# A transformer step on one core: another order of loading, modulating and norming at its beginning

## The chip, the core and the metric

One core of a Trainium2 chip runs the whole step as one program. The metric is the device time of one execution in microseconds; the kernel before took 1898.06 us, the median of three executions. The engines are TensorE (PE, with its weight loads as PEld), VectorE (DVE), ScalarE (ACT), GpSimd (POOL) and SyncE (SP), which here issues the DMAs.

## The reference, cut to what matters

640 tokens of width 1024 (512 latent, 128 context) go through two layers. Each layer begins with a norm that is modulated by vectors computed from a conditioning, one for the latent tokens (`c`) and one for the context tokens (`c_ctx`):

```
def modulation(cond, w_ada, b_ada):
    m = jax.nn.silu(cond) @ w_ada + b_ada          # (6 * 1024)
    return m.reshape(cond.shape[0], 6, D_MODEL)

def modulate(x, g, shift, scale):
    return rms_norm(x, g) * (1 + scale[:, None, :]) + shift[:, None, :]

hp = modulate(xp, g[0], mc[:, 0], mc[:, 1])
hs = modulate(xs, g[0], ml[:, 0], ml[:, 1])
...   # h @ w_in (1024 x 3584), retention and attention heads, @ w_out, MLP; then layer 1
```

The change concerns the part up to the first tiles of `h @ w_in`: shift and scale of layer 0, which are the first 2048 columns of `w_ada[0]`, the first norm, and `h` itself.

## The kernel before

Activations are kept transposed: `xT` has eight tiles `k` (feature groups of 128 on the partitions) by 640 tokens, and tokens are worked in two halves `s` of 320; the second half holds 192 latent and 128 context tokens, so its modulation has two pieces (`HALVES`). Every large matmul is done in float32 by three passes: an operand is split into `hi` (a rounding copy) and `lo` (the difference), and `unit` (lines 733 to 752) adds `lo*hi`, `hi*lo`, `hi*hi` over the eight `k` for both halves, 48 matmuls of 320 columns a unit. Weights come in pieces of 512 KB into four stage buffers (`load_piece`), ACT makes `w_hi` (`act_split`, line 535), DVE `w_lo` (`dve_split`, line 544). Stage "ac" has 20 such units; piece `n + 2` is split once unit `n` is done, since two slots hold the split pieces. Beside these units DVE accumulates the later modulation vectors from `w_ada` slabs (`ada_ops`, lines 1945 and 1948), and PE sums them over partitions (`sum_rows`, line 788: four matmuls of 32 columns of weights and 512 moving columns, one for each 32-column group of the array).

The program of each engine is written out by hand, so the order on an engine is the order of the text. The beginning is:

- SP issues the constants and small vectors, three 1 MB loads of `w_ada` (`load_ada`, line 554; 256 columns of all 1024 rows, so rows of 1 KB), the tokens `xtok` (lines 635, 636), five more loads of `w_ada` as the ring of three comes free, then the first four pieces, two slabs and, after the last ada step, the table `dist`.
- PE transposes the small vectors, does `ada_step(0..2)` (eight matmuls of two weight columns, `csil`, by 256 moving columns each, line 822; a small transpose of the result follows, `turn_mod`, line 812), then the 40 transposes of the tokens (line 840), ada steps 3 to 5, the sums of squares of half 0 (`sum_squares`, lines 761 and 765), step 6, those of half 1, step 7, and `spread_root` for both (line 775). Then come the units.
- ACT copies each step's result (`mod_rows`, line 1424), squares the tiles (line 1357), takes the roots (line 1364), splits pieces 0 and 1, and does `first_operand` (line 1369).
- DVE copies the transposed tokens (lines 1969, 1971), adds the bias to each step's columns (`mod_columns`, line 1913), splits pieces 0 and 1, and then does `first_modulate` for each `k` and both halves in turn (lines 1851 and 1854).
- POOL adds the squares (line 2465) and makes the low part of each tile (`first_low`, line 2469).

In unit 0 `both_ready` makes PE wait for tile `k` of both halves. Later norms ("in0m", "in1", "in1m") work by halves with `modulate` on DVE, `operand` on ACT and `low` on DVE, beside other units.

Of the kernel before, what the change touches and what calls it, by code (L numbers as in the profile page):

```python
# [19 lines left out]
P = 128  # L20
D = 1024
# [181 lines left out]
ADA_W = 256  # L203
N_ADA = 2 * 6 * D // ADA_W
ADA_RING = 3
ADA_START = 8
# [42 lines left out]
def build(nc, i, o):  # L249

    top = ExitStack()
    with top:
# [64 lines left out]

        [ada_a] = lay(64, ("ada_a", [P, ADA_RING, KD, ADA_W], F32))
        [modrow_a] = lay(130, ("modrow_a", [2, 2, ADA_W], F32))

# [58 lines left out]
        ada_in = [sem(f"ada_in{n}") for n in range(ADA_RING)]  # L379
# [110 lines left out]
        def norm_place(name, s, k):  # L490

            n = 2 * (k % 2) + s if name == "in0" else k % 4
            return nt[:, n // 2, HALF * (n % 2):HALF * (n % 2 + 1)]
# [56 lines left out]

        def load_ada(queue, n):

            src = i["w_ada"][0].rearrange("(k p) m -> p k m", p=P)
            queue.dma_start(ada_a[:, n % ADA_RING], src[:, :, ADA_W * n:ADA_W * (n + 1)])\
                .then_inc(ada_in[n % ADA_RING], 16)
# [27 lines left out]
        def _(sp):  # L583
# [64 lines left out]
            sp.wait_ge(ada_done, ADA_START)  # L648
# [69 lines left out]
        def _(pe):  # L718
# [14 lines left out]
            def unit(name, u, k_tiles, m, x_hi, x_lo, ready=None, base=0, wide=None, beside=None):  # L733

                wide = wide or m
                g, n, (_, only) = UNIT_AT[name] + u, PIECE_AT[name] + unit_piece(name, u), unit_tile(name, u)
                pe.wait_ge(w_lo_done, n + 1)
# [3 lines left out]
                for j, k in enumerate(range(k_tiles)):  # L741
# [4 lines left out]
                    for s in range(2) if only is None else (only,):  # L746
# [5 lines left out]
                last.then_inc(unit_done, 1)  # L752
# [53 lines left out]
            def turn_mod(n):  # L806
                pe.wait_ge(modrow_done, n + 1)
                if n >= 2:
                    pe.wait_ge(mod_out, n - 1)
                modrow = modrow_a  # L810
                for j in range(2):
# [4 lines left out]
            def ada_step(n):  # L816
# [8 lines left out]
                if n:  # L825
                    turn_mod(n - 1)
# [1846 lines left out]
```

## Time and profile before

| | |
|---|---|
| median of three executions | 1898.06 us (1897.71 to 1900.3) |
| the profiled execution | 1896.75 us, span 1895.0 us |
| mean granted TensorE clock | 0.959 |
| busy in the span | PE 94%, DVE 57%, ACT 39%, POOL 12% |
| first tile of the first norm starts on DVE | 60.77 us |
| unit 0 done, unit 1 done | 84.7 us, 92.6 us |

The profiled execution is one execution; its span is measured from the first to the last instruction, and 1.75 us of its time lie around the span. Times in the rows below are microseconds from the span's start. A busy share is an average over stages with different limits; for a change at the beginning the rows of the beginning count, and what comes after only tells whether a shift is kept. A wait is put down to the semaphore that came last.

### The profile page before, as it was taken

To read this page: it belongs to the slowest core of one execution; us is meant where nothing else is said; L and a number is where in the kernel's file an instruction comes from. 1 tells how busy PE (TensorE), PEld (TensorE's weight loads), DVE (VectorE), ACT (ScalarE), POOL (GpSimd) and SP (SyncE) were. 2 spreads that over 40 slices of the span, in tenths; PEclk is the share of its full clock that TensorE was granted. 3 is DMA by queue.
4 is the path that set the end of the run, shared out by engine and by line. 5 is a ranking of instruction groups with operands and counts; after the bars stand their busy time and mean duration, and the time that the engine had idled before them with its cause. 6 is when DMAs were issued, how large, how long until landed. Compare 5 with 4: busy or idle time off the path is not lost.

```text
span 1895.0 us, 27246 instructions
## 1 busy us (share of the span) xinstructions
PE 1776.7 (94%) x11072; PEld 1568.8 (83%) x11072; DVE 1080.2 (57%) x1716; ACT 734.1 (39%) x1235; POOL 224.5 (12%) x234
## 2 busy tenths in 40 slices
PE   7799997789999999999998998999899999999997
PEld 3699872358999999999998996333699999999997
DVE  2567836763556677777454655566555673342345
ACT  1323215364554321312334464555446532131232
POOL 1300000142200000000121030333221000000012
PEclk9799999889999999999997998999999999999998
DMA  8354322103236546555310030000314552222231
GB/s 270 102 168 155 111 67 67 34 1 90 64 104 185 171 122 193 150 159 154 98 43 25 26 109 1 1 1 1 112 34 123 177 147 78 77 69 78 79 90 56
DMA packets 262447, 179.46 MB, mean 95 GB/s; under 512 B 12862, under 2 KB 236979, under 8 KB 262323
## 3 DMA queue, kind: packets, MB, share of 16 engines
q1 hardware_dynamic: 262322, 177.72, 32.1%
q8 instruction: 88, 1.44, 0.3%
q14 instruction: 37, 0.30, 0.1%
HBM read 174.15 MB, written 3.62 MB: 94 GB/s over the span
## 4 chain that ended last, share of the span: by engine, by line
PE 84%; DVE 6%; ACT 4%; issue 3%; POOL 2%; DMA 0%; SPq 0%; DVEq 0%; ACTq 0%; POOLq 0%
PE ps L749 22%; PE ps L751 21%; PE ps L750 21%; PE ps L1268 3%; PE ps L822 2%; PE ps L1278 2%; PE ps L765 1%; PE ps L883 1%; PE ps L884 1%; PE ps L885 1%; PE ps L775 1%; PE ps L1179 1%; PE ps L761 1%; ACT km L1715 1%; PE ps L897 1%
## 5 line engine op out<-in xcount | busy, mean ns | idle before, releaser
L535 ACT ACTIVATE w_hi<-stage 128x1024 fp32r<-128x1024 f32 (+1 forms) x177 | 185.5, 1050 | 679.2 <-PE ps L751 550.3
L544 DVE TENSOR_TENSOR w_lo<-stage,w_hi 128x1024 fp32r<-128x1024 f32 (+1 forms) x177 | 218.4, 1236 | 341.1 <-ACT w_hi L535 340.9
L749 PE MATMUL ps<-hM_hi,w_lo 128*128 128x320 f32 x960 | 300.9, 313 | 2.4 <-DVE hM_lo L1879 2.4
L750 PE MATMUL ps<-hM_lo,w_hi 128*128 128x320 f32 x960 | 299.0, 311 | 0.0
L751 PE MATMUL ps<-hM_hi,w_hi 128*128 128x320 f32 x960 | 299.0, 311 | 0.0
L749 PE MATMUL ps<-h_hi,w_lo 128*128 128x320 f32 x824 | 257.8, 313 | 2.6 <-DVE h_lo L2262 2.6
L750 PE MATMUL ps<-h_lo,w_hi 128*128 128x320 f32 x824 | 256.2, 311 | 0.0
L751 PE MATMUL ps<-h_hi,w_hi 128*128 128x320 f32 x824 | 256.1, 311 | 0.0
L2465 POOL TENSOR_TENSOR rstd<-rstd,sq 128x320 f32<-128x320 f32 x80 | 80.6, 1014 | 1046.9 <-ACT sq L1357 1044.1
L749 PEld LDWEIGHTS ps<-hM_hi,w_lo 128*128 128x128 f32 x960 | 182.5, 190 | 6.8 <-DVE hM_lo L1879 3.5
L750 PEld LDWEIGHTS ps<-hM_lo,w_hi 128*128 128x128 f32 x960 | 182.5, 190 | 0.0
L751 PEld LDWEIGHTS ps<-hM_hi,w_hi 128*128 128x128 f32 x960 | 182.4, 190 | 0.0
L749 PEld LDWEIGHTS ps<-h_hi,w_lo 128*128 128x128 f32 x824 | 156.3, 190 | 6.6 <-DVE h_lo L2262 3.7
L750 PEld LDWEIGHTS ps<-h_lo,w_hi 128*128 128x128 f32 x824 | 156.3, 190 | 0.0
L751 PEld LDWEIGHTS ps<-h_hi,w_hi 128*128 128x128 f32 x824 | 156.2, 190 | 0.0
L1948 DVE SCALAR_TENSOR_TENSOR acc_mlp<-slab_mlp,csil,acc_mlp 128x512 f32<-128x512 f32 x196 | 134.5, 745 | 0.0
L749 PE MATMUL ps<-hA_hi,w_lo 128*128 128x320 f32 x320 | 103.4, 323 | 9.9 <-POOL hA_lo L2469 9.9
L2245 DVE TENSOR_TENSOR yT<-yT,ps 128x640 f32<-128x640 f32 (+1 forms) x64 | 41.8, 653 | 123.1 <-PE ps L751 122.5
L750 PE MATMUL ps<-hA_lo,w_hi 128*128 128x320 f32 x320 | 101.8, 318 | 0.0
L751 PE MATMUL ps<-hA_hi,w_hi 128*128 128x320 f32 x320 | 101.8, 318 | 0.0
L2355 DVE TENSOR_REDUCE w_lo<-ps 128x1 fp32r<-128x640 f32 x64 | 52.1, 814 | 66.5 <-PE ps L1180 46.1
L1767 ACT ACTIVATE pT<-ps 128x512 f32<-128x512 f32 x84 | 50.0, 596 | 76.5 <-PE ps L1268 73.9
(363 smaller groups left out, 3606.7 us busy)
## 6 DMA issues: line engine op xcount, KB each, us to landing
stage<-in_w_mlp_out SPq DMA_DIRECT2D x83, 512.0 KB, 4.4
stage<-in_w_mlp_in SPq DMA_DIRECT2D x80, 512.0 KB, 4.3
slab_mlp<-in_w_ada SPq DMA_DIRECT2D x28, 1024.0 KB, 5.3
stage<-in_w_in_ac SPq DMA_DIRECT2D x28, 512.0 KB, 3.8
slab_ac<-in_w_ada SPq DMA_DIRECT2D x12, 1024.0 KB, 6.5
ada_a<-in_w_ada SPq DMA_DIRECT2D x8, 1024.0 KB, 8.1
stage<-in_w_out_ac SPq DMA_DIRECT2D x8, 512.0 KB, 4.4
stage<-in_w_out_c SPq DMA_DIRECT2D x8, 512.0 KB, 4.1
```

Of the source, the lines that this page charges most:

```text
L535: nc.scalar.activation(hi_place(n)[:, 0:width], stage[:, n % STAGE, 0:width], ACT.Copy)\
L544: nc.vector.tensor_tensor(lo_place(n)[:, 0:width], stage[:, n % STAGE, 0:width], hi_place(n)[:, 0:width].bitcast(F32), ALU.subtract).then_ ...
L749: mm(out, lo[:, k], xh, start=j == 0, stop=False)
L750: mm(out, hi[:, k], xl, start=False, stop=False)
L751: last = mm(out, hi[:, k], xh, start=False, stop=j == k_tiles - 1)
L822: last = mm(ps[0:2, n % 2, 0:ADA_W], csil[:, k, :], slot[:, k, :], start=k == 0, stop=k == KD - 1)
L1268: mm(ps[:, 2 + n % 2, :], km[0:97, h, P * kb:P * (kb + 1)], q, start=True, stop=True).then_inc(m_s, 1)
L1767: f(pT[:, n % P_RING, :], ps[:, 2 + n % 2, :], ACT.Exp).then_inc(m_e, 1)
L1948: last = stt(acc, w, c, acc, ALU.mult, ALU.add)
L2245: tt(y_, y_, p_, ALU.add).then_inc(dve_evac, 1)
L2355: nc.vector.tensor_reduce(peak[p % 2][:, 96 + j:97 + j], src, AX.X, ALU.max, negate=True).then_inc(a_max, 1)
L2465: sub(rstd[:, half(s)], rstd[:, half(s)], sq[:, k % 2, half(s)], ALU.add).then_inc(added[s], 1)
```

## The change

- SP: the tokens are issued right behind the small vectors. Then come eight loads of `w_ada`, one for each `k`: 128 rows of 2048 columns (8 KB a row), 1 MB each, each with its own semaphore and place, no ring. The four first pieces follow, then the small decay inputs, the slabs, and `dist`, which waits for nothing now.
- PE: the tokens' transposes come first. `ada_step(k)` is four matmuls, one for each 32-column group, with 32 weight columns (`cwide`: two used, thirty zero) and 512 moving columns, accumulated over `k` in one bank. Steps 0 to 5 stand behind the transposes, 6 and 7 between the sums and the spreads. Then four 128x128 transposes turn the whole result at once.
- ACT makes one copy of 128x512 where it made eight of 2x256; the squares of both halves stand one behind the other; the second piece's split stands behind tile 3 of half 0.
- DVE: one `first_columns` in place of eight `mod_columns`. The first norm's tiles go by halves with the functions of the later norms; `first_modulate`, `first_operand`, `first_low` go. Split 0 stands behind the second tile, split 1 behind the sixth. Before half 1, DVE waits for its own eight low parts of half 0.
- PE does unit 0 and unit 1 of stage "ac" for half 0, then both for half 1 (`part`).
- POOL gains one memset (`cwide`) and loses sixteen subtractions.

The diff, without lines that follow from these:

```diff
-            for n in range(ADA_RING):
-                load_ada(sp, n)
             sp.dma_start(xtok[:, 0:NB, :], i["x_sample"][0].rearrange("(b p) d -> p b d", p=P)).then_inc(x_in, 16)
             sp.dma_start(xtok[:, NB, :], i["x_prompt"][0]).then_inc(x_in, 16)
+            for k in range(KD):
+                sp.dma_start(ada_a[:, k, :], i["w_ada"][0, P * k:P * (k + 1), 0:4 * GRP]).then_inc(ada_in[k], 16)
+            for j in range(STAGE):
+                load_piece("ac", j)
...
-            for n in range(ADA_RING, ADA_START):
-                sp.wait_ge(ada_done, n - ADA_RING + 1)
-                load_ada(sp, n)
-            for j in range(STAGE):
-                load_piece("ac", j)
             load_slab(0)
             load_slab(1)
             table_rows()
-            sp.wait_ge(ada_done, ADA_START)
...
+            def ada_step(k):
+                pe.wait_ge(ada_in[k], 16)
+                for j in range(4):
+                    last = mm(ps[32 * j:32 * j + 32, 0, :], cwide[:, k, :], ada_a[:, k, GRP * j:GRP * (j + 1)],
                               start=k == 0, stop=k == KD - 1)
+                if k == KD - 1:
+                    last.then_inc(ada_done, 1)
...
+            pe.wait_ge(c_ready, 1)
+            for k in range(6):
+                ada_step(k)
             pe.wait_ge(x_out, 10)
-            ada_step(5)
             sum_squares("in0", 0)
             ada_step(6)
             sum_squares("in0", 1)
+            spread_root("in0", 0)
             ada_step(7)
-            spread_root("in0", 0)
             spread_root("in0", 1)
+            pe.wait_ge(modrow_done, 1)
+            for n in range(4):
+                last = nc.tensor.transpose(ps[:, 1, P * n:P * (n + 1)], modrow_a[:, P * n:P * (n + 1)], ident[:])
+            last.then_inc(mod_t, 1)
...
-            for j in range(20):
-                unit("ac", j, KD, P, hA_hi, hA_lo, ready=both_ready if j == 0 else None)
+            for s in range(2):
+                for j in range(2):
+                    unit("ac", j, KD, P, hA_hi, hA_lo, ready=h_ready("in0", s) if j == 0 else None, part=s)
+            for j in range(2, 20):
+                unit("ac", j, KD, P, hA_hi, hA_lo)
...
             square_root("in0", 0, D)
             square_root("in0", 1, D)
-            mod_rows(7)
+            act.wait_ge(ada_done, 1)
+            f(modrow_a[:], ps[:, 0, :], ACT.Copy).then_inc(modrow_done, 1)
             act_split(act, 0)
-            act_split(act, 1)
             for k in range(KD):
-                for s in range(2):
-                    first_operand(s, k)
+                operand("in0", 0, k)
+                if k == 3:
+                    act_split(act, 1)
+            for k in range(KD):
+                operand("in0", 1, k)
...
+            first_columns()
+            modulate("in0", 0, 0)
+            modulate("in0", 0, 1)
             dve_split(dve, 0)
-            dve_split(dve, 1)
+            low("in0", 0, 0)
+            for k in range(2, KD):
+                modulate("in0", 0, k)
+                low("in0", 0, k - 1)
+                if k == 5:
+                    dve_split(dve, 1)
+            low("in0", 0, KD - 1)
+            dve.wait_ge(h_lo_done[0], KD)
             for k in range(KD):
-                for s in range(2):
-                    first_modulate(s, k)
+                modulate("in0", 1, k)
+                if k:
+                    low("in0", 1, k - 1)
+            low("in0", 1, KD - 1)
```

## Rows read from the trace of the kernel before

**Rows 1.** The page: busy time of the engines and their share of the span.
```profile
PE 1776.7 (94%) x11072; PEld 1568.8 (83%) x11072; DVE 1080.2 (57%) x1716; ACT 734.1 (39%) x1235; POOL 224.5 (12%) x234
```
**Rows 2.** Windows: length; busy (count) of PE, PEld, DVE, ACT, POOL; granted clock, DMA, GB/s.
```profile
65.00:82.70 17.70, 13.58 (x42) 11.01 (x43) 15.63 (x32) 6.12 (x13) 12.89 (x14) 0.50 0.01 3
82.70:86.50 3.80, 3.80 (x14) 3.80 (x15) 0.67 (x1) 1.65 (x2) 0.00 (x0) 0.50 0.00 0
...
160.00:200.00 40.00, 40.00 (x276) 38.96 (x275) 31.59 (x45) 11.49 (x15) 0.00 (x0) 1.00 0.51 159
```
**Rows 3.** Timeline: start, duration, engine, line, operation; first tile, splits behind units 0, 1.
```profile
60.77 0.48 DVE L1851 TENSOR_TENSOR nt<-xT,ps 128x320 f32<-128x320 f32 x1
...
84.74 1.06 ACT L535 ACTIVATE w_hi<-stage 128x1024 fp32r<-128x1024 f32 x1 [3.12 <-PE ps L751]
...
92.67 1.06 ACT L535 ACTIVATE w_hi<-stage 128x1024 fp32r<-128x1024 f32 x1 [6.28 <-PE ps L751]
```
**Rows 4.** Groups by line and form, DVE, 60 to 84: busy us, mean ns.
```profile
L1854 DVE TENSOR_SCALAR nt<-nt,coef,mod 128x128 f32<-128x128 f32 x8 | 7.1, 884 | 0.0
```
**Rows 5.** The chain that ended last, 30 to 66 us: start, duration, what.
```profile
44.66 1.65 PE ps L765 x12
...
53.49 3.56 PE ps L822 x16
...
58.49 2.36 DVE w_lo L544 x2
```
**Rows 6.** Timeline of SP's DMA issues, and the landing times of xtok's two.
```profile
3.74 2.46 SPq L554 DMA_DIRECT2D ada_a<-in_w_ada  x3
6.24 3.06 SPq L635 DMA_DIRECT2D xtok<-in_x_sample  x1
...
DMA to landing us min/median/max: 12.7/13.5/14.3
```
**Rows 7.** Windows as in rows 2: ada rows, token rows, pieces of 512-byte rows.
```profile
8.00:14.00 6.00, 4.45 (x11) 1.39 (x12) 0.00 (x0) 0.00 (x0) 0.00 (x0) 1.00 1.09 349
14.00:20.00 6.00, 6.00 (x27) 2.25 (x26) 0.23 (x2) 0.75 (x2) 0.00 (x0) 1.00 1.04 407
...
42.00:48.00 6.00, 4.14 (x23) 2.96 (x24) 0.00 (x0) 3.44 (x9) 4.01 (x5) 0.80 1.20 293
```
**Rows 8.** Timeline: the tokens' first transposes and the last two copies.
```profile
23.11 2.51 PE L840 MATMUL ps<-ident,xtok 128*128 128x128 f32 x20
...
31.25 1.26 DVE L1971 COPY xT<-ps 128x512 f32<-128x512 f32 x2
```
**Rows 9.** Timeline of ACT: first and last square of half 1, then the table load.
```profile
44.39 0.45 ACT L1357 ACTIVATE rstd<-xT 128x320 f32<-128x320 f32 x1
...
50.18 0.47 ACT L1357 ACTIVATE sq<-xT 128x320 f32<-128x320 f32 x1 [0.54 <-POOL rstd L2465]
...
51.61 1.28 ACT L1364 ACT_TABLE_LOAD   x1
```
**Rows 10.** Timeline of PE: `sum_rows`, between units and after a pause.
```profile
141.79 1.07 PE L788 MATMUL ps<-acc_ac,ones 128*32 128x512 f32 x8
...
226.08 1.62 PE L788 MATMUL ps<-acc_ac,ones 128*32 128x512 f32 x8 [3.52 <-issue]
```
**Rows 11.** Timeline: a later `spread_root`; and the page: a copy-like activation from PSUM.
```profile
537.86 1.54 PE L775 MATMUL ps<-ident,rs 128*128 128x128 f32 x6 [2.57 <-DVE rs L1828]
...
L1767 ACT ACTIVATE pT<-ps 128x512 f32<-128x512 f32 x84 | 50.0, 596 | 76.5 <-PE ps L1268 73.9
```
**Rows 12.** Timeline of a later norm: half 0's tile pace on DVE, half 1's on ACT.
```profile
499.31 0.54 DVE L1866 SCALAR_TENSOR_TENSOR nt<-xT,coef,ps 128x320 f32<-128x320 f32 x1
...
500.24 0.54 DVE L1866 SCALAR_TENSOR_TENSOR nt<-xT,coef,ps 128x320 f32<-128x320 f32 x1
...
545.99 0.92 ACT L1383 ACTIVATE nt<-nt,mod,coef 128x192 f32<-128x192 f32 x2
546.95 0.47 ACT L1387 ACTIVATE hM_hi<-nt 128x320 fp32r<-128x320 f32 x1
```

More of the change, by code:

```diff
@@ L202 @@
 P_RING = 8
[L203 to L206, printed above, removed]
+ADA_START = 1
 GRP = 512
@@ L378, in build @@
         const_in, rows_in, x_in = sem("const_in"), sem("rows_in"), sem("x_in")
-        ada_in = [sem(f"ada_in{n}") for n in range(ADA_RING)]
+        ada_in = [sem(f"ada_in{k}") for k in range(KD)]
+        csil_zero = sem("csil_zero")
         decay_in, dist_in = sem("decay_in"), sem("dist_in")
@@ L731, in free_pair, with unit @@
                         pe.wait_ge(dve_evac, d)
-            def unit(name, u, k_tiles, m, x_hi, x_lo, ready=None, base=0, wide=None, beside=None):
+            def unit(name, u, k_tiles, m, x_hi, x_lo, ready=None, base=0, wide=None, beside=None, part=None):
                 wide = wide or m
                 g, n, (_, only) = UNIT_AT[name] + u, PIECE_AT[name] + unit_piece(name, u), unit_tile(name, u)
+                halves = (0, 1) if only is None and part is None else (only if part is None else part,)
                 pe.wait_ge(w_lo_done, n + 1)
@@ L745, in unit @@
                         ready(k, j)
-                    for s in range(2) if only is None else (only,):
+                    for s in halves:
                         out = ps[0:m, first_bank(g) + (s if only is None else 0), 0:HALF]
@@ L751, in unit @@
                         last = mm(out, hi[:, k], xh, start=False, stop=j == k_tiles - 1)
-                last.then_inc(unit_done, 1)
+                if part != 0:
+                    last.then_inc(unit_done, 1)
             def sum_squares(name, s):
@@ L1365, in square_root @@
                     .then_inc(root_done[s], 1)
[L1367 to L1369 removed]
             def operand(name, s, k):
                 layer, which, shift = MODULATED[name]
[L1375 removed]
+                place, out = norm_place(name, s, k), hA_hi if name == "in0" else hM_hi
                 act.wait_ge(h_full[s], KD * MOD_NO[name] + k + 1)
                 if s == 0:
[L1378 removed]
+                    f(out[:, k, half(0)], place, ACT.Identity, bias=mod[:, layer, 8 * shift + k, 0:1])\
                         .then_inc(h_hi_done[0], 1)
@@ L1385, in operand @@
                 last.then_inc(affine_done, 1)
-                act.wait_ge(affine_done, KD * (MOD_NO[name] - 1) + k + 1)
-                f(hM_hi[:, k, half(1)], place, ACT.Copy).then_inc(h_hi_done[1], 1)
+                act.wait_ge(affine_done, KD * MOD_NO[name] + k + 1)
+                f(out[:, k, half(1)], place, ACT.Copy).then_inc(h_hi_done[1], 1)
             def y_square(name, stage, u):
@@ L1843, in residual @@
                 tt(xT[:, k, cols], xT[:, k, cols], place, ALU.add).then_inc(x_done[s], 1)
-            def first_modulate(s, k):
-                dve.wait_ge(rstd_done[s], 1)
-                if k >= 2:
-                    dve.wait_ge(h_lo_done[s], k - 1)
-                place = norm_place("in0", s, k)
-                link(tt(place, xT[:, k, half(s)], spread("in0", s), ALU.mult))
-                for a, b, g in HALVES[s]:
-                    part = place[:, a - HALF * s:b - HALF * s]
-                    last = ts(part, part, coef[:, 0, A1, k, g:g + 1], mod[:, 0, 8 * SHIFT1 + k, g:g + 1],
-                              ALU.mult, ALU.add)
-                last.then_inc(h_full[s], 1)
             def modulate(name, s, k):
@@ L1957, in _ @@
             link(nc.vector.reciprocal(cexp[:], cexp[:]))
+            dve.wait_ge(csil_zero, 1)
+            for g in range(2):
+                tt(cwide[:, :, g], vecT[:, ROW_C + 8 * g:ROW_C + 8 * g + 8], cexp[:, 8 * g:8 * g + 8], ALU.mult)
             for g in range(2):
@@ L2474, in _ @@
                     add_square("in0", s, k)
-            for k in range(KD):
-                for s in range(2):
-                    first_low(s, k)
             pool.wait_ge(v_done, 8)
```

91 lines of the change are left out of this document (17 added, 74 removed).

## The prediction

> **What bounds the kernel now.** I read the page first: TensorE (PE) is busy 94% of the span [rows 1]. Then the windows by stage: a steady stretch behind the beginning has PE busy 40.00 of 40 us, at the full clock, with 276 matmuls (0.145 us each), while DVE has room (31.59) [rows 2]. The change touches only what lies ahead of it. So from the third projection unit on, the kernel is PE-bound, and whatever the beginning saves shifts everything behind it. The stretch to price ends when unit "ac" 1 ends: ACT starts piece 3's split, which waits for exactly that, at 92.67; unit 0 ended before 84.74 [rows 3].
>
> Next the timeline and the chain, backwards from 92.6. Units 0 and 1 hold 96 matmuls; at 0.145 they need 14 us, but unit 0 alone takes from 65 to 84.6. It waits, tile by tile, for the DVE, ACT, GpSimd round of `first_modulate`, `first_operand`, `first_low`, and since PE pauses it holds the lower level: granted clock 0.50 (1.2 GHz) from 65 to 86.5, busy 13.58 of 17.70 us [rows 2]. A 128-column `tensor_scalar` of this round takes 0.884 us while GpSimd works [rows 4]. In front of the round, first tile at 60.77 [rows 3], stands a chain of four ada steps behind the squares, the last of 3.56 us, and then two splits on DVE (2.36 us) [rows 5]. Before that, PE could start only when tokens landed: they are queued behind 3 MB of modulation weights and land 12.7 to 14.3 us after their issues, the first at 6.24 [rows 6].
>
> **Part 1, tokens first.** The token issue takes the place of the first ada issue, 3.74 instead of 6.24 [rows 6], and nothing large is ahead of it. 4 KB rows (14 to 20 us) came at 407 GB/s, 1 KB rows (8 to 14) at 349 [rows 7]. 2.6 MB plus the small vectors at 407 take 6.7 us from about 4.7, plus about 1 us until a semaphore is seen (the first 5.4 MB at these rates end near 19.7 and the tokens' landing reads 20.5): 12.4. At 349 it would be 13.6. The ten groups of transposes and their copies are DVE-bound; from the first transpose at 23.11 to the last copy's end at 32.51 [rows 8] they take 9.4 us; PE may be at the slow level, which costs the first group 0.3: xT is ready at 22.2.
>
> The Trainium skill ("DMA: Bandwidth & Descriptors", Specifications) gives about 358 GB/s as a core's limit from HBM. The trace moves 407 in a six-microsecond stretch [rows 7], so the measurement decides; by the page's figure the tokens would land 1.1 us later and the time would be about 2 us higher than my forecast.
>
> **Part 2, squares.** They no longer wait for ada rows. One half takes 6.3 us, from the first square at 44.39 to the end of the last at 50.65, bound by GpSimd's adds between them [rows 9]. Two halves back to back: 22.2 + 12.6 = 34.8. ACT's table load of 1.28 follows (as at 51.61) [rows 9]: 36.1; square root and reciprocal 0.4: 36.5.
>
> **Part 3, modulation vectors.** Removed: 8 steps of 8 matmuls, 8 small copies, 16 small transposes. Added: 8 steps of 4 matmuls with 32 weight columns each, in four column groups. The nearest row is `sum_rows`, same shape and groups: its 4 matmuls (8 records) last 1.07 us, and 1.62 in a stretch at the slow level [rows 10]. Streamed one behind the other, the same 2048 columns are the old step, 3.56 [rows 5]. I take 1.0 to 1.6 a step. Rows of 8 KB should come no slower than 4 KB ones: 2.6 us for 1 MB, the last at 12.4 + 8 x 2.6 = 33.2 (36.4 or later at 349, with the later tokens 37.6). PE is in order: transposes until 22, steps 0 to 5 until 29.6 (row 5 lands at 28), sums 0, step 6, sums 1 (2.2 us each; their later part takes 1.65) [rows 5] until about 35.3, so ACT's squares and table load end last, not DMA. Then, in a line: spread 0 from 36.5, 1.0 (1.54 for such six records at the slow level) [rows 11], to 37.6; step 7, 1.3, to 38.9; ACT's copy of 128x512, 0.6 [rows 11], beside spread 1, to 39.9; four transposes, 0.5 to 1.0 with what a hand-over costs (20 take 2.51 at the full clock) [rows 8], to 40.8; two adds and two coefficients on DVE, 0.7, first `modulate` at 41.5, against 60.77: 19.3 us saved so far. ACT's first split comes behind the copy and is hidden beside the transposes; its piece lands behind all ada rows and about 1.8 us (512 KB at 293) [rows 7] later, at 35 to 39.5. SP's queue passes eight 1 MB issues before pieces 0 to 3, the decay vectors, slabs and `dist`; the last of 16 MB has landed by 53 even at 293, and the slabs' first reader comes at 68.
>
> **Part 4, tiles by halves.** Half 0 is later layers' pattern: one modulate plus one low per tile, 0.93 us (499.31 to 500.24) [rows 12]. Two modulates, split 0 (1.15), low: 2.6. Six pairs 5.6, split 1 1.15, last low 0.5: 9.9 us; unit 0's first half runs along, and unit 1's first half, which the old order had no room for, starts then. The new self-wait before half 1 holds DVE for about 0.1, nothing is queued behind it but these tiles. Half 1 is ACT-bound: two affine pieces and a copy, 545.99 to 547.42, 1.43 a tile [rows 12]; 0.5 + 8 x 1.43 + 0.7 = 12.6. Total 22.5 us against 21.8 in the old round: this part saves nothing on the tiles themselves. It saves behind them, since half of unit 1 is already done. After the last tile 27 matmuls are left instead of 51. In the old round PE, once fed without pause, stood at 0.50 for 3.8 us more (82.7 to 86.5, 14 matmuls) [rows 2]; so 14 in 3.8 us and 13 at 0.145: 5.7 us. Unit 1 ends at 41.5 + 22.5 + 5.7 = 69.7.
>
> Is the next unit ready? Unit 0 is done near 65; ACT's split and DVE's, 2.5 us, end at 67.5, and the bank's copy is done by then: PE goes on without a gap. GpSimd loses 16 operations that nobody misses.
>
> **Sum.** 92.6 - 69.7 = 22.9 us. The profiled execution took 1896.75 us (span 1895.0): 1873.9. It stands 1.3 below the median of 1898.06; with that, 1875.2. Unknowns: DMA at 349 throughout delays sums 1 and step 7 and costs 3; a full clock from the ada steps on would give 1.4 before the tiles and 1.7 after them, a slow one costs 1.2 before them; one tile of half 1 waiting longer costs under 2; where the clock falls and rises later, about 1 either way. Down they add up to 4.1, up to 6.2 or 7: 1871 to 1881.5.
>
> **Rivals.** (a) *The head comes out slower than its rows*: the long rows arrive at 293 GB/s like the pieces [rows 7], PE does steps late, tiles take one wait more each: 6 to 10 us less gain, 1881.5 to 1885. Against it: rates grow with the row length in this trace. (b) *Column groups do not run side by side*: PE is the bound. Steps run back to back from 22.2, ada is done at 22.2 + 5.4 + 8d, against 38.9. With d = 3.6: 17.5 us lost, gain 5.4, 1892.7. (c) *The other side*: the same, at the slow level. Zero gain is at d = 4.3 us a step; with 7.1 (2 x 3.56) it is 1898.06 + 22.6 = 1920.7. Against (b) and (c): 1.07 and 1.62 us in [rows 10]; for them only that the old beginning has no such matmul. (d) *The gain is real but is given back*: a stage that waits for a transfer with a fixed time. All later loads wait on progress, not on time, and the beginning's are landed 20 us before their readers: 1897 to 1899.
>
> **Chances.** Forecast 0.85 (of which 0.05 below 1871, with the fast clock), (a) 0.08, (b) 0.02, (c) 0.03, (d) 0.02. The range holds about 0.80. Something like 0.2% (3.8 us) is what a measurement of this kernel can tell from no change. Faster by more: 0.95; same: 0.02; slower: 0.03.
>
> **What would show it.** In the profile after: x_sample lands near 12, last xT copy ends near 22; groups of 8 ada records last 1.0 to 1.7 us and wait for DMA; last square ends near 35; first modulate near 41.5; low of half 0 paces 0.93, half 1 1.43; the split of piece 3 starts at 69.7 instead of 92.67, and PE is full from there on. A last ada row after 38, ada groups of 3 us and more, or PE gaps between units 1 and 3 would make me wrong.

## The result and the profile after

The changed kernel took 1882.42 us (median of five, 1874.76 to 1883.39), the kernel before 1899.59 us beside it; the ratio is 0.9905 with a 95% interval of 0.9885 to 0.9925. It is faster by 17 to 18 us, not by 22.9, and 0.9 us slower than the upper end of the range. The profiled execution took 1881.38 us. Of the runs below, one execution of the run both took 1992.44 us at a mean granted clock of 0.82, where all others have 0.955 to 0.965; it is left out of every figure.

The page of after, for [rows 1]: engines' busy time, and the queue that brings the engines' own instructions, which [rows 1] does not show; its line is the same in both. (Its columns: packets, MB, share of 16 engines.)
```profile
PE 1756.4 (93%) x10996; PEld 1562.0 (83%) x10996; DVE 1073.5 (57%) x1696; ACT 738.8 (39%) x1244; POOL 209.7 (11%) x219
...
q8 instruction: 88, 1.44, 0.3%
```
The timeline of after from the tokens' landing to the first tile, for [rows 5, 6, 8, 9, 11]: start, duration, engine, line, operation.
```profile
13.05 4.83 PE L814 MATMUL ps<-ident,xtok 128*128 128x128 f32 x28 [7.26 <-DMA xtok<-in_x_prompt]
...
21.68 1.27 DVE L1925 COPY xT<-ps 128x512 f32<-128x512 f32 x2
...
25.48 1.06 PE L802 MATMUL ps<-ada_a,cwide 128*32 128x512 f32 x8 [1.24 <-DMA ada_a<-in_w_ada]
...
27.97 1.06 PE L802 MATMUL ps<-ada_a,cwide 128*32 128x512 f32 x8 [1.42 <-DMA ada_a<-in_w_ada]
...
32.08 1.93 PE L802 MATMUL ps<-ada_a,cwide 128*32 128x512 f32 x8
...
35.17 1.41 PE L753 MATMUL ps<-ones,rstd 128*128 128x1 f32 x6 [1.15 <-POOL rstd L2424]
35.54 1.28 ACT L1341 ACT_TABLE_LOAD   x1
36.44 2.70 PE L757 MATMUL ps<-ones,sq 128*128 128x1 f32 x12
...
39.00 1.52 PE L767 MATMUL ps<-ident,rs 128*128 128x128 f32 x6
...
40.45 1.94 PE L802 MATMUL ps<-ada_a,cwide 128*32 128x512 f32 x8
42.32 1.45 PE L767 MATMUL ps<-ident,rs 128*128 128x128 f32 x6
...
43.60 0.61 PE L829 MATMUL ps<-ident,modrow_a 128*128 128x128 f32 x4
...
44.82 1.01 DVE L1818 SCALAR_TENSOR_TENSOR nt<-xT,coef,ps 128x320 f32<-128x320 f32 x2
```
The reader sees a beginning that runs 0.7 us behind the forecast up to the last square (xT ready at 22.95, forecast 22.2; table load at 35.54, forecast 34.8) and then loses 2.6 us more, so that the first tile starts 3.3 us late (44.82, forecast 41.5): from 35.17 to 44.2 one TensorE operation follows another, each at nearly twice its short duration (an ada step is 1.06 at 26 and 28, and 1.93 at 32 and 40). The windows of after, for [rows 2, 7], say why: length; busy (count) of PE, PEld, DVE, ACT, POOL; granted clock, DMA, GB/s.
```profile
16.00:32.00 16.00, 12.52 (x94) 7.14 (x92) 6.95 (x9) 5.09 (x12) 6.02 (x7) 0.93 1.00 417
...
30.00:42.00 12.00, 10.85 (x51) 7.66 (x50) 0.35 (x2) 4.58 (x10) 4.31 (x5) 0.50 1.07 292
42.00:46.00 4.00, 2.21 (x14) 1.66 (x10) 1.68 (x7) 2.15 (x4) 0.00 (x0) 0.81 1.05 396
46.00:57.00 11.00, 8.51 (x28) 7.18 (x29) 9.60 (x18) 5.86 (x12) 0.00 (x0) 0.54 0.43 139
57.00:70.00 13.00, 10.51 (x56) 9.22 (x56) 7.43 (x15) 10.78 (x24) 0.00 (x0) 0.89 0.01 2
```
The granted clock is 0.50 (1.2 GHz) for the whole stretch 30 to 42. (The clock's own records begin only at 16.2 us in after and at 14.8 in before, and the windows read 1.00 ahead of them, as the first one of [rows 7] does. How fast TensorE runs there has to be read from durations, see before_fill below.) The tiles follow: half 0 from 44.82 to 55.11, half 1 to 66.9, and the split behind unit 1 at 72.78 (timeline of ACT), for [rows 3, 12]:
```profile
60.95 0.92 ACT L1356 ACTIVATE nt<-nt,mod,coef 128x192 f32<-128x192 f32 x2
...
62.28 0.92 ACT L1356 ACTIVATE nt<-nt,mod,coef 128x192 f32<-128x192 f32 x2
...
72.78 1.06 ACT L534 ACTIVATE w_hi<-stage 128x1024 fp32r<-128x1024 f32 x1 [3.33 <-PE ps L742]
```
Unit 1 ends 19.9 us earlier than before, but the span is only 15.4 us shorter (1895.0 less 1879.6). So 4.5 us go behind the beginning. ACT's weight splits are the same in every kernel here, so the n-th split serves as a milestone. The table holds, for each kernel run, how much earlier than in the kernel before it starts (us; the head row is that split's time in the trace of before). It is worked out from the start times in the timelines. Each row is one execution, and executions of one kernel differ: after's five go from 1874.76 to 1883.39. By the span of its trace both_again is 28.0 us faster than before, by medians 22.5; order 13.6 and 17.4. So the rows tell where something is lost or gained in that execution, and the medians what a kernel takes.

| kernel | unit 1's end (92.7) | 289.9 | 544.7 | 691.3 | 702.6 | 721.1 | 851.1 | 1327.7 | 1352.6 | 1857.2 | span |
|---|---|---|---|---|---|---|---|---|---|---|---|
| after | 19.9 | 19.8 | 21.8 | 21.8 | 20.6 | 18.9 | 19.7 | 18.5 | 17.0 | 16.4 | 15.4 |
| same_again | 19.9 | 19.8 | 22.0 | 22.0 | 20.6 | 19.3 | 19.9 | 18.8 | 17.2 | 16.7 | 15.7 |
| order | 20.8 | 20.7 | 20.8 | 20.8 | 19.7 | 18.5 | 19.2 | 16.8 | 15.2 | 14.7 | 13.6 |
| group_by_group | 19.1 | 19.1 | 19.1 | 19.2 | 17.7 | 17.0 | 17.6 | 15.7 | 15.7 | 15.7 | 14.7 |
| early_fill | 18.7 | 18.6 | 18.6 | 18.7 | 18.7 | 18.6 | 18.7 | 21.4 | 19.9 | 19.3 | 19.3 |
| order_fill | 24.0 | 22.8 | 24.1 | 24.1 | 24.1 | 24.1 | 24.1 | 24.1 | 22.6 | 22.0 | 22.0 |
| warm | 21.9 | 20.6 | 21.9 | 22.0 | 22.0 | 22.0 | 22.0 | 22.6 | 22.6 | 22.6 | 22.6 |
| both_again | 25.6 | 25.4 | 27.3 | 27.4 | 27.4 | 27.3 | 27.4 | 27.9 | 27.9 | 28.0 | 28.0 |
| halves_only | 4.9 | 4.7 | 4.6 | 4.6 | 4.7 | 4.5 | 4.7 | 4.6 | 4.6 | 4.6 | 4.6 |
| rows_1k | 7.9 | 7.8 | 7.7 | 7.7 | 7.0 | 6.0 | 6.6 | 7.0 | 5.4 | 4.9 | 3.9 |
| before_fill | -7.2 | -8.5 | -7.3 | -7.3 | -8.5 | -9.6 | -8.8 | -10.1 | -10.1 | -10.1 | -11.1 |

### The profile page after: what moved, and what is told of

The parts are those of the page before. It is cut to its first block, busy times and chain, and to the rows that moved or that the text cites. A ratio compares the mean times of both kernels' runs of the same rounds, so it can differ in the third digit from the quotient of the medians.

```text
span 1879.6 us, 27040 instructions
## 1 busy us (share of the span) xinstructions
PE 1756.4 (93%) x10996; PEld 1562.0 (83%) x10996; DVE 1073.5 (57%) x1696; ACT 738.8 (39%) x1244; POOL 209.7 (11%) x219
## 4 chain that ended last, share of the span: by engine, by line
PE 81%; DVE 7%; ACT 5%; issue 3%; POOL 2%; DMA 2%; SPq 0%; DVEq 0%; ACTq 0%; POOLq 0%
PE ps L740 21%; PE ps L742 20%; PE ps L741 20%; PE ps L1245 3%; PE ps L1255 2%; PE ps L757 1%; DMA stage<-in_w_mlp_out 1%; PE ps L860 1%; PE ps L862 1%; PE ps L861 1%; PE ps L767 1%; DVE w_lo L543 1%; PE ps L1156 1%; POOL rstd L2424 1%; ACT w_hi L534 1%
## 6 DMA issues: line engine op xcount, KB each, us to landing
ada_a<-in_w_ada SPq DMA_DIRECT2D x8, 1024.0 KB, 17.6
```

## The experiments

Two questions: why did the head come out 3 us short (the clock, or the order of the last steps), and what takes 4.5 us behind it although nothing there was edited?

**same_again: the kernel after, unedited.** 

> The changed kernel once more, unedited. Theory A (what the beginning saves is fixed, what follows scatters): the split of piece 3 starts at 72.8 us again within 0.2, 19.9 us earlier than in the kernel before, while the total comes 15 to 22 us below the kernel before and the difference between the two numbers sits in other stretches of the MLPs than in the first profile. Rival B (the change itself costs something later, always in the same place): the same stretches lose the same 4 to 5 us again, near 680 to 720, 1030 to 1080 and 1310 to 1340 us, and the total stays 15 to 17 us below.

Measured: 1882.13 us, ratio 0.991 (0.9895 to 0.9924). The row of the table repeats the one of after within 0.4 us at every milestone. In both traces the later loss sits in the same places, which speaks for the program and against scatter. It need not hold for every execution: one of after's five, which was not traced, took 1874.76 us at a mean granted clock of 0.962 (the others 0.957 to 0.959).

**warm: fillers that keep TensorE at work.** `keep_warm(n)` does `n` matmuls of 256 moving columns into a free bank; nobody reads them.
```diff
             for k in range(6):
                 ada_step(k)
+                keep_warm({3: 4, 4: 3}.get(k, 0))
             pe.wait_ge(x_out, 10)
             sum_squares("in0", 0)
             ada_step(6)
+            keep_warm(6)
```


> The changed kernel with 13 filler matmuls of 256 columns on PE, results unused: four behind ada step 3, three behind step 4, six behind step 6, where PE waits for rows or squares. Theory A (PE falls to 1.2 GHz at 30 us because the short ada steps leave it idle, and the sums, spreads and the last step are then done at half speed): granted clock stays 1.00 until 40, the 18 sum records of half 1 take 2.2 us instead of 4.0, each spread 0.8 instead of 1.4, step 7 1.1 instead of 1.9; first modulate at 41.2 to 41.8 instead of 44.8, split of piece 3 near 69.5, total 3 to 3.5 us below the changed kernel. Rival B (the clock is not what made the chain late; the order of the waits is): first modulate stays within 0.5 us of 44.8. Rival C: the fillers stand in the way, first modulate at 46 or later.

Measured: 1873.68 us, ratio 0.9867 (0.9851 to 0.9884). Its window of the ada steps, then its timeline of PE:
```profile
20.00:30.00 10.00, 9.93 (x70) 4.54 (x70) 3.00 (x5) 4.13 (x10) 4.32 (x5) 1.00 1.01 422
```
```profile
32.73 4.54 PE L810 MATMUL ps<-xtok,ident 128*128 128x256 f32 x12
...
37.11 0.72 PE L753 MATMUL ps<-ones,rstd 128*128 128x1 f32 x6
37.70 1.48 PE L757 MATMUL ps<-ones,sq 128*128 128x1 f32 x12
```
With PE busy 9.93 of 10 us the clock stays at 1.00, and the sums take 2.1 us in place of 4.0. The last six fillers are too many: they hold the sums back until 37.11, and the clock falls twice on the way, so the first tile comes at 44.37, only 0.45 earlier, where 41.2 to 41.8 was expected. Two more windows of warm:
```profile
32.00:34.00 2.00, 2.00 (x12) 1.13 (x5) 0.00 (x0) 0.94 (x2) 1.71 (x3) 0.81 1.17 309
34.00:36.00 2.00, 2.00 (x6) 1.55 (x6) 0.00 (x0) 1.34 (x3) 0.94 (x2) 0.50 1.21 294
```
The clock fell here although PE was busy without a pause from 24 on. So work on TensorE put the fall off, from 30 to 33, and did not rule it out. Unit 1's end gains 2.0 us, most of it under the tiles. What had not been expected: this kernel also loses nothing in the first MLP.

**order: the last steps in another order.**
```diff
             ada_step(6)
+            ada_step(7)
             sum_squares("in0", 1)
             spread_root("in0", 0)
-            ada_step(7)
-            spread_root("in0", 1)
             pe.wait_ge(modrow_done, 1)
             for n in range(4):
                 last = nc.tensor.transpose(ps[:, 1, P * n:P * (n + 1)], modrow_a[:, P * n:P * (n + 1)], ident[:])
             last.then_inc(mod_t, 1)
+            spread_root("in0", 1)
...
             square_root("in0", 0, D)
-            square_root("in0", 1, D)
             act.wait_ge(ada_done, 1)
             f(modrow_a[:], ps[:, 0, :], ACT.Copy).then_inc(modrow_done, 1)
+            square_root("in0", 1, D)
```


> The changed kernel with another order only: on PE step 7 stands before the sums of half 1, and the four transposes before spread 1; on ACT the copy of the modulation row stands between the two roots. Nothing is added or left out. Theory A (sums 1, spread 0, step 7, copy, transposes form one serial chain of PE work, so whatever is taken out of it counts in full): step 7 (1.9 us) and spread 1 (1.4 us, hidden beside the copy so far by 0.6) leave the chain, sums 1 end about 0.7 later since step 7 ends near 35.9; first modulate at 42 to 42.8 instead of 44.8, total 2 to 2.8 us less. Rival B (another wait is just behind: the last ada row or ACT): first modulate at 44 or later and the total within 1 us.

Measured: 1880.45 us, ratio 0.9903 (0.9886 to 0.992); unit 1 ends 0.9 us earlier than in after, the first tile 0.7 (44.10). The first tile was expected at 42 to 42.8. The clock is at 0.50 through all of it, and step 7 now delays the sums of half 1 by 2.1 us (37.25 for 35.17), so moving steps off the chain gains only a part. A window of order, and its timeline of the last sums:
```profile
30.00:42.00 12.00, 12.00 (x56) 9.01 (x57) 0.35 (x2) 5.67 (x12) 4.31 (x5) 0.50 1.01 274
```
```profile
37.25 1.44 PE L753 MATMUL ps<-ones,rstd 128*128 128x1 f32 x6
38.55 2.70 PE L757 MATMUL ps<-ones,sq 128*128 128x1 f32 x12
```

**halves_only: the kernel before with part 4 alone** (the first norm's tiles by halves, `part` units, nothing of the loads or ada steps).

> The kernel before with the fourth part of the change alone: the first norm by halves on DVE and ACT, splits 0 and 1 inside it, units 0 and 1 of stage ac half by half; loading, ada steps and squares as before. Theory A (my part 4: tiles as long as before, gain behind them): first modulate near 58.5 instead of 60.8 since the splits no longer stand in front, last tile of half 1 22.1 us later, 5.8 us for what is left of units 0 and 1: split of piece 3 at 86.4 instead of 92.7, total 6.3 us below the kernel before (1892 to 1894). Rival B (the halves bring nothing that the slow clock does not take back): within 2 us of the kernel before, so that all of the 19.9 us would come from loading and ada steps. Rival C (GpSimd was the brake, tiles get much shorter): more than 9 us less.

Measured: 1891.8 us, ratio 0.9957 (0.9943 to 0.9972). Unit 1 ends 4.9 us earlier, kept to the end. The first tile was expected at 58.5, since the splits no longer stand in front, and starts at 61.39, 0.6 later than before: the last two old ada steps start 1.0 us later than in before (54.41 for 53.42) and take 5.3 us in place of 3.6, with the clock at 0.67 over 54 to 56 and at 0.50 over 56 to 58. From the first tile to unit 1's end this kernel needs 5.5 us less than before. Of after's 19.9 us, 15.95 are the earlier first tile (60.77 to 44.82), and the other 3.9 come behind it, with part 4.

**group_by_group: steps 0 to 3 with the column groups outermost.**
```diff
-            for k in range(6):
+            for k in range(4):
+                pe.wait_ge(ada_in[k], 16)
+            for j in range(4):
+                for k in range(4):
+                    mm(ps[32 * j:32 * j + 32, 0, :], cwide[:, k, :], ada_a[:, k, GRP * j:GRP * (j + 1)],
+                       start=k == 0, stop=False)
+            for k in range(4, 6):
                 ada_step(k)
```


> The changed kernel with ada steps 0 to 3 in another order: four matmuls one behind the other in the same column group, then the next group, so that neighbours never lie in different groups. Same work and result. Theory A (the four groups work side by side only when neighbouring matmuls lie in different ones): the 32 records take about 13.7 us (0.43 each) instead of 3.64, the rest of the beginning moves up by 6 to 8 us. Rival B (32 weight columns alone make such a matmul short): 3.6 us as before.

Measured: 1882.1 us, one execution. The timeline of group_by_group first, then of order_fill (below), whose steps 0 to 3 are those of after:
```profile
23.29 9.12 PE L822 MATMUL ps<-ada_a,cwide 128*32 128x512 f32 x29 [2.42 <-DMA ada_a<-in_w_ada]
```
```profile
20.75 3.64 PE L804 MATMUL ps<-ada_a,cwide 128*32 128x512 f32 x32
```
The same 32 records take 3.64 us when neighbours lie in different column groups and about 10 when they lie in one (23.29 to 33.7 with the three that the row leaves out; the clock is 0.84 over 23 to 34). Theory A had 13.7, so the overlap does not go entirely, but most of it does: the groups run side by side if the order of the instructions alternates between them. At 2.6 us a step this is still short of the 3.6 of rival (b). The head is only 0.8 us worse, not 6 to 8: the clock is low just from 23 to 27 and then at 1.00 until 40, where after has 0.50.

**early_fill: 52 short instructions ahead of everything.** By now three kernels lost 1.1 to 1.7 us twice in the first MLP (splits at 702.6 and 721.1) and two did not (warm, halves_only), with nothing edited there. What differs is the number of TensorE instructions ahead. They come by DMA too, in the profile page's 88 packets of the instruction queue, 16 KB each; so an instruction more or less moves all later packets against the work.
```diff
             nc.tensor.transpose(ps[:, 5, 0:96], brow[:], ident[0:96, 0:96]).then_inc(rows_t, 1)
+            for _ in range(13):
+                mm(ps[:, 2, 0:8], ident[:], ident[:, 0:8], start=True, stop=True)
```


> The changed kernel with 13 small filler matmuls (8 columns, 52 PE instructions with their weight loads, results unused) right behind the transposes of the small vectors, at 5.5 us, where PE has nothing to do until 13. They change neither the clock nor the chain at the beginning, only the count of PE instructions, and by as much as the fillers of run warm. Theory A (the page counts 88 packets of 16 KB for instructions; where one of them comes while a weight piece is awaited, the piece lands 1 to 1.7 us later; the change has 171 PE instructions fewer, which moves these packets onto the pieces awaited in the first MLP): piece 3's split at 72.8 as before, pieces 79 and 82 split about 22 us earlier than in the kernel before instead of 20.6 and 18.9, and the total 1876 to 1879. Rival B (run warm gained its later 4 us by the clock or by chance): the pieces lose the same 1.2 and 1.7 us again, total 1880 to 1883.

Measured: 1878.05 us, ratio 0.9896 (0.9879 to 0.9913). They run while PE waits for the tokens; unit 1's end is 1.2 us later than in after, and the loss in the MLP is gone (18.7, 18.7, 18.6). The medians alone would not show it (0.9896 and after's 0.9905 lie within each other's intervals); the milestones do. In after the two pieces behind that wait land 7.96 us after their issue (674.11 to 682.07), in early_fill 6.69 (677.25 to 683.94). The chain of after, the timeline of SP and ACT of after, then the same timeline of early_fill:
```profile
674.11 7.94 DMA stage<-in_w_mlp_out
```
```profile
674.11 1.42 SPq L583 DMA_DIRECT2D stage<-in_w_mlp_out  x2
...
682.07 1.06 ACT L534 ACTIVATE w_hi<-stage 128x1024 fp32r<-128x1024 f32 x1 [11.53 <-DMA stage<-in_w_mlp_out]
```
```profile
677.25 1.13 SPq L583 DMA_DIRECT2D stage<-in_w_mlp_out  x2
...
683.94 1.06 ACT L534 ACTIVATE w_hi<-stage 128x1024 fp32r<-128x1024 f32 x1 [10.27 <-DMA stage<-in_w_mlp_out]
```
And the DMA queues (packets, MB, share of 16 engines) of one microsecond in after, 677 to 678, in the midst of that transfer:
```profile
q1 hardware_dynamic: 201, 0.39, 99.6%
q8 instruction: 1, 0.02, 6.3%
```
Sixteen engines carry the piece, and one of them spends this microsecond (6.3% of sixteen) on the instruction packet. A piece is there when its last rows are. The Trainium skill ("Runtime: NRT & Kernel Launch", Instruction fetch mechanics) says that an engine's instructions are refilled in blocks of 16 KiB, 256 instructions, through a queue of its own, at a cost that is mostly hidden. The trace agrees on the size; here the cost is not TensorE's but that of the load beside it. Counted from the split at 691.3, the packet comes at +7.8 in after, +8.5 in same_again, +8.3 in order, +9.0 in group_by_group and +5.4 in rows_1k, all of which lose 0.7 to 1.5 us at 702.6 while the pieces are in flight from +4.6; it comes at +2.0 in early_fill, order_fill and both_again, at +2.1 in warm, at +12.4 in before and at -3.2 in halves_only, none of which lose. The next piece behind it, issued at about +24, shows the same once more. The chain of after:
```profile
694.11 8.00 DMA stage<-in_w_mlp_out
```
Where a packet comes at +25.0 to +27.7 (after, same_again, order, group_by_group, rows_1k and before_fill, below), this piece lands 7.0 to 8.0 us after its issue and the split at 721.1 loses 0.6 to 1.7 us more; where it comes at +22.5 or earlier, or at +30.5 or later, the piece lands after 6.4 to 6.6.

**before_fill: the kernel before with 84 such instructions** (21 matmuls), which puts its packets where after has them.
```diff
+            for _ in range(21):
+                mm(ps[:, 6, 0:8], ident[:], ident[:, 0:8], start=True, stop=True)
```


> The kernel before with 21 such small fillers (84 PE instructions) at 5.5 us, which PE would have spent waiting. 84 more leaves the instruction packets where 171 fewer leave them (one packet holds 256 instructions). Theory A: beginning and split of piece 3 as before (92.7), but piece 79 and piece 82 of the first MLP land 1.2 and 1.7 us later than in the kernel before, and the total is 1 to 3 us above it. Rival B (nothing to do with instruction packets): equal to the kernel before within 1 us.

Measured: 1907.85 us, ratio 1.0049 (1.0031 to 1.0067). The fillers were expected to be free and were not; the timeline of PE:
```profile
5.63 9.02 PE L805 MATMUL ps<-ident 128*128 128x8 f32 x42
```
42 records at 0.213 us each, at a moment when the old PE order had its first ada steps coming: the tokens' transposes start 4.2 us later (27.26 for 23.11), and unit 1 ends 7.2 us later, since steps 6 and 7 then meet the lower clock (5.8 and 5.1 us for 4.9 and 3.6). The weight loads say why a record of 8 columns takes so long: each takes 333 ns. So does each of the sums' loads in after, with the clock at 0.50 (its row follows), and in both_again, at 1.00, one takes 192 ns (the row at 36.47, below).
```profile
36.37 2.68 PEld L757 LDWEIGHTS ps<-ones,sq 128*128 128x128 f32 x12
```
So by its durations TensorE is at the lower level in the first 14 us of before_fill, where the clock's records have not begun. But the point of the run holds: with the packet at +8.7 the kernel before, which has nothing of the change, loses 1.2 and 1.1 us at the two pieces of the MLP (-7.3, -8.5, -9.6).

**both and both_again: the reordered head, 9 wide fillers, 4 narrow ones** (order's edit, `keep_warm` of 4 and 3 behind steps 3 and 4 and of 2 behind step 7, and 4 of early_fill's). 

> The changed kernel with the order of run order, four fillers of 256 columns behind ada step 3, three behind step 4 and two behind step 7, and four small ones at 5.5 us, 52 PE instructions in all. Theory A (order and clock each take their part out of one serial chain, and the count of instructions keeps the packets off the awaited pieces): granted clock 1.00 until about 40, sums 1 end at 38, first modulate at 40 to 40.8, split of piece 3 near 67.5, total 1870 to 1873, 9 to 12 us below the changed kernel. Rival B (something else ends last once PE is faster: squares, table load): first modulate at 42 or later, total 1874 or more.

Measured: 1874.74 us (median of three), ratio 0.9875 (0.9854 to 0.9896), above the 1870 to 1873 expected. Its trace is that of the execution at 1992.44 us and is not read; both_again is the same kernel.

> The kernel of the run 'both' once more, to have an undisturbed trace of it: 9 wide filler matmuls keep the clock up, the reordered head, and 52 more instructions. Theory: sums 1 ends near 37.5, first modulate near 42, unit 1 ends at 69.5 to 70.5 (shift 22 to 23), the first MLP loses nothing, median 1873 to 1875.5. Rival (keeping the clock up is worth nothing once the order is right, since the order run already got 0.9 of it): unit 1 ends near 71.9 and the median is 1877 to 1878, as with the short fillers.

Measured: 1874.3 us (four executions, 1868.82 to 1874.85), ratio 0.9878 (0.9862 to 0.9895); the profiled one is the fastest by 5 us, span 1867.0. A window and then the timeline:
```profile
30.00:40.00 10.00, 9.26 (x71) 7.35 (x68) 0.35 (x2) 6.09 (x12) 4.32 (x5) 0.90 1.13 291
```
```profile
33.95 1.07 PE L804 MATMUL ps<-ada_a,cwide 128*32 128x512 f32 x8 [0.74 <-DMA ada_a<-in_w_ada]
...
35.91 0.72 PE L753 MATMUL ps<-ones,rstd 128*128 128x1 f32 x6
36.47 1.42 PEld L757 LDWEIGHTS ps<-ones,sq 128*128 128x128 f32 x12
...
40.66 1.00 DVE L1827 SCALAR_TENSOR_TENSOR nt<-xT,coef,ps 128x320 f32<-128x320 f32 x2
...
67.09 1.06 ACT L534 ACTIVATE w_hi<-stage 128x1024 fp32r<-128x1024 f32 x1 [1.86 <-PE ps L742]
```
With the clock at 0.90 in the stretch where after has 0.50, the first tile starts at 40.66, before my forecast of 41.5, and unit 1 ends 25.6 us earlier than before: the head that the prediction had drawn is there once PE has its full clock for longer and the order keeps step 7 off the chain.

**order_fill: the reordered head with early_fill's 52 instructions.**

> The reordered head (step 7 ahead of the last sums, transposes ahead of the second spread) together with the 52 short TensorE instructions at 5.5 us. Theory A (the later loss in the first MLP is only the place of the instruction packets): unit 1 ends 19.6 us earlier than before (18.7 with the fillers alone, 0.9 more from the order), pieces 79 to 82 of the first MLP lose nothing, median 1877 to 1878, ratio 0.988 to 0.990. Rival B (the later loss in the order run comes from the reordering): 1.2 us and more are lost at those pieces again and the median stays at 1880 or above.

Measured: 1875.33 us, ratio 0.9884 (0.9866 to 0.9902). Nothing is lost in the first MLP (24.1 throughout): theory A again. But unit 1 ends 24.0 us earlier, where 19.6 was expected from the sum of the two edits. The windows of order and then of order_fill, over the tiles:
```profile
42.00:70.00 28.00, 23.03 (x99) 20.72 (x99) 19.03 (x40) 17.75 (x36) 0.00 (x0) 0.64 0.35 121
```
```profile
42.00:70.00 28.00, 21.52 (x113) 19.06 (x112) 21.05 (x42) 18.61 (x37) 0.00 (x0) 0.83 0.40 132
```
The programs are the same from 12 us on; the clock is 0.83 against 0.64. It first returns to 1.00 at about 38 in order_fill and at about 58 in order. So equal instructions after nearly equal pauses can be granted different clocks, worth 3.2 us here. What decides it no run shows.

**rows_1k: the eight loads as column blocks, rows of 1 KB.**
```diff
-                sp.dma_start(ada_a[:, k, :], i["w_ada"][0, P * k:P * (k + 1), 0:4 * GRP]).then_inc(ada_in[k], 16)
+                cols = slice(256 * k, 256 * (k + 1))
+                sp.dma_start(ada_a[:, :, cols], i["w_ada"][0, :, cols].rearrange("(k p) n -> p k n", p=P)).then_inc(ada_in[k], 16)
...
+            for k in range(8):
+                pe.wait_ge(ada_in[k], 16)
```


> The kernel after with its 8 MB of modulation weights loaded in eight column blocks of all 1024 rows (rows of 1 KB, as before) in place of rows of 8 KB; since each step then needs all eight blocks, step 0 waits for all of them. Theory (the long rows are worth a higher rate): from 12.4 us the 8 MB come at about 350 GB/s and the last lands near 36.5 to 37.5 in place of about 33, the sums stand behind it, unit 1 ends 3 to 6 us later than after, one time 1885 to 1889. Rival (the rate in the beginning does not depend on the rows): the last lands at 33 to 34, the sums of half 1 are only 2 us or less later, one time 1883 to 1885.

Measured: 1892.91 us, one execution. The windows of rows_1k, to be set beside 417 GB/s over 16 to 32 us in after:
```profile
16.00:36.00 20.00, 4.43 (x29) 3.64 (x27) 7.23 (x9) 7.18 (x17) 8.57 (x10) 0.71 1.09 348
```
The last block lands at 37.6, against 33.9 for the last of the long rows (the DMA wait of both_again's step 7 ends there). Rate and landing are as the theory said; the time is 4 us above its range, because I had not counted that six steps at 7.18 us in all now stand between the landing and the sums (unit 1's end: 12.0 us later than after, of which 3.7 are the landing). The long rows pay twice: by the rate, and since each row block is one step's input, by letting seven steps run while the rest lands.

## Why the prediction was wrong

The direction, the mechanism and most of the head were right; the time fell outside the range, for two reasons.

*Tokens first* (forecast: landed 12.4, xT 22.2): 13.05 and 22.95; right within 0.75 us. *Squares* (table load done 36.1): 36.82, right. *DMA rate*: 417 GB/s with 8 KB rows over 16 to 32 us, a little over the 407 I took; "such rows come no slower" held. The Trainium skill ("DMA: Bandwidth & Descriptors", Specifications) gives about 358 GB/s as a core's limit from HBM. The trace does not agree: it moves 417. (For the tokens at that figure the prediction has 1.1 us more; 6.7 x 407 / 358 gives 0.9.)

*A step takes 1.0 to 1.6 us*: 1.06 at the full clock, 1.93 at 1.2 GHz, so the upper bound from [rows 10] was too low: that row's 1.62 was a stretch partly at the full clock.

*"Sums 1 ... until about 35.3, so ACT's squares and table load end last"* is the first step that failed. The 35.3 is PE's work laid end to end from 29.6 (2.2, 1.3, 2.2), as if the sums of half 1 waited for nothing. They wait for the squares, and the prediction's own last square ends at 34.8: even their later part of 1.65 would have ended at 36.45, not 35.3. In fact all 18 records stand behind the last add of GpSimd (35.03), so nothing of them is hidden, and at 0.50 they take 4.0 us: done at 39.1. ACT's root and DVE's reciprocal for spread 0 were done at 37.3, so PE's sums ended last. Spread 0 starts at 39.0 instead of 36.5; 0.7 of this are the squares' own delay and 1.8 the sums. Then spread 0 took 1.5 instead of 1.1 and step 7 1.9 instead of 1.3, and the rest of the chain took what was forecast. The prediction named the level as an unknown: 1.4 us less before the tiles at the full clock, 1.2 more at the slow one, 2.6 between the two. The runs put the difference at about 3.5 (first tile at 44.82, in both_again at 40.66, less the 0.7 that the order alone gives); this is an estimate, since it takes the two edits to add up. The irony is that the change made it: with short steps that wait for the next row (7.3 of 10 us busy from 20 to 30) the clock falls at 30, where with the old, slower steps it was at 1.00 until about 45.

*Tiles* (22.5 us): 22.1, right; half 0 10.3 for 9.9, half 1 at 1.33 a tile for 1.43. *5.7 us for the rest*: 5.9. So the 3.0 us missing at unit 1 were all there at the first tile: 0.7 by the squares, 2.6 between 35 and 44.8, and 0.3 came back under the tiles. Rival (a), a head 6 to 10 us slower, was wrong: rates were high, and the tiles had no wait more. That the time lies in its range of 1881.5 to 1885 is chance, since the head gave less than half of what is missing. (b) and (c) were wrong: a step takes 1.06 or 1.93 us, and group_by_group shows that it rests on the order of the matmuls.

*"All later loads wait on progress, not on time"* is the second step that failed. It is true of the program's own loads, and yet it left out the transfers that nobody writes: the instruction packets. Their place depends on the number of instructions ahead, 76 matmuls fewer by the page, and in after two of them fall into transfers that PE is waiting for. Net of what comes back by 851, that costs 2.1 us. At the very end it costs once more: from the start of ACT's last copy to the end of the span it is 8.4 us in after (1871.17 to 1879.6) and 7.4 in order_fill (1865.57 to 1873.0), and after has a packet at 1874.1, inside the last stores; all six kernels with after's or before_fill's packets lose this 1.0 us between 1857.2 and the span's end, and no other does. That this packet is the cause is a reading of the trace; no run moved it alone. Rival (d) had the sign of it, but as "a transfer with a fixed time" it was the wrong mechanism, and 0.02 was too little for "something is given back".

*The clock once more.* Between the splits at 1327.7 and 1352.6 after loses another 1.5 us. Both kernels have the same pause of PE there, waiting for GpSimd, and the same work behind it. Windows of the pause and of what follows, of before and then of after:
```profile
1344.00:1347.60 3.60, 0.31 (x3) 0.04 (x1) 1.75 (x3) 1.68 (x2) 1.54 (x1) 1.00 0.01 2
1347.60:1353.00 5.40, 5.36 (x36) 5.36 (x37) 3.43 (x3) 3.75 (x7) 0.52 (x1) 1.00 0.42 116
```
```profile
1325.50:1329.10 3.60, 0.27 (x3) 0.01 (x2) 1.75 (x3) 1.68 (x2) 1.53 (x1) 1.00 0.00 0
1329.10:1334.50 5.40, 5.40 (x26) 5.40 (x27) 3.39 (x3) 2.65 (x4) 0.00 (x0) 0.68 0.39 109
```
The interval between the two splits has only two values in the twelve traces: 24.85 us in before, warm, halves_only, both_again, before_fill and group_by_group, and 26.38 or 26.39 in after, same_again, order, order_fill, early_fill and rows_1k. The same pause is followed by a slow stretch or is not; what decides is open. The +2.0 us between 289.9 and 544.7 in after (same 1406 matmuls in both, PE busy 215.5 us in before and 212.9 in after) and the -1.1 between 851 and 1328 are of this kind too, by their PE times, but no run isolates them.

The account by spans: 22.9 forecast; -3.0 in the head; +1.9 up to 691; -2.1 in the first MLP; -1.1 and -0.6 in places not settled; -1.5 at 1330; -1.0 in the last stores; together 15.4. By medians the gain is 17.2: the profiled execution of before is 2.8 us below the median measured beside after (1899.59; the prediction reckoned with 1.3, from 1898.06), and that of after 1.0 below its own.

The versions to keep are warm, both_again and order_fill: 24.2, 22.5 and 21.5 us under the kernel before by medians of the same chip. Their ratios (0.9867, 0.9878, 0.9884) lie within each other's intervals, so the runs do not rank them; order_fill needs no wide fillers.

## What to carry to other kernels

Where a change turns long steps into short ones that wait for data, read the granted clock of that stretch as part of the change: price the chain behind it at the lower level too, and read in a trace whether work put in between helps (it put the fall off by 3 us in warm and by 8 in both_again, whose window 30 to 40 has 0.90). An operation placed "behind" its producer counts whole, not from its middle: ask which semaphore its first instruction waits for. And a gain at the beginning shifts the instruction packets against all later work: a stage that is waiting for loads is not safe merely because nothing in it was edited, and a few idle instructions early on can win back a microsecond or two there, if they stand where TensorE waits anyway.

## What the runs showed of the hardware

- Four matmuls of 32 weight columns and 512 moving columns, in four column groups, take 1.06 us at the full clock when they alternate (after); 32 records in group-by-group order take about 10 us in place of 3.64, at a clock of 0.84.
- An instruction packet of 16 KB holds one of the sixteen DMA engines for about 1 us (median 1.10, from 0.88 to 2.18 in the twelve traces), and awaited pieces of 512 KB came 0.6 to 1.7 us later when one fell in their flight.
- A matmul with 8 moving columns is not short when each brings its own weights: 0.213 us a record at the beginning of the kernel, where a load of 128 columns of weights takes 333 ns. With one moving column at the full clock a record takes 0.12 us and the load 192 ns (both_again).
- Until 13.7 to 18.1 us (by the trace) the profile has no record of the clock and its windows read 1.00, while the weight loads take the 333 ns of the lower level.
- TensorE's clock fell from 1.00 to 0.50 at 33 us in warm with PE busy 2.00 of every 2 us since 24.
- Rows of 8 KB came at 417 GB/s, rows of 1 KB at 348, in the same place of the same program, without idle engines in either.
- The same pause of 3.3 us on TensorE is followed by the full clock or by a stretch at 1.2 GHz that costs 1.5 us. after and same_again, one program traced twice, gave the same value.
